# Two transformer blocks on one core: from one common order of steps to an order for each engine

## The chip, the cores and the metric

The kernel runs on one core of a Trainium2 chip. The core has TensorE (PE in the views; its weight loads are PEld), VectorE (DVE), ScalarE (ACT), GpSimd (POOL), and SyncE (SP), which here only issues DMAs. The engines run their own instruction streams and meet at semaphores. The metric is the device time of one execution in microseconds (us); less is better.

## The reference

Input is one sequence of 256 tokens with 2048 channels, all in fp32, which goes through two blocks. The first mixes with sparse attention (NSA: compressed, selected and window branches, 8 query heads, 2 key heads) and a gated DeltaNet (8 heads), merges the two, and ends in a feed-forward net (FFN). The second mixes with RWKV7 (16 heads of 64) and latent attention (MLA, 8 heads), and ends in an FFN with a convolution in its gate. Cut to the steps that matter:

```python
# block 1
h = rms_norm(x, norm1_w);  proj = h @ w_in
o_nsa = nsa_mixer(q, kv, gates)                # 3 branches, softmax each
o_dn  = gated_deltanet(qkv, z, a, beta)        # conv of 4 taps, silu, l2norm, chunks, triangular solve
mixed = g_nsa * (o_nsa @ w_up_nsa) + g_dn * (o_dn @ w_up_dn)
x = x + mixed @ w_o
x = x + (silu(h2 @ w_gate) * (h2 @ w_up)) @ w_down;  x = rms_norm(x, norm_f_w)
# block 2
proj = rms_norm(x) @ w_in_2
y = concat(rwkv7_mixer(...), mla_mixer(...))   # a recurrence; softmax attention
x = x + y @ w_out
x = x + (silu(conv3(h @ w_gate)) * (h @ w_up)) @ w_down;  return rms_norm(x)
```

## The kernel before

**Main stream.** All weights pass once through a ring of 6 blocks of 128 x 1024 fp32 elements. ACT copies the high part of each block (`split`, L1413, recorded at the helper's L1290), DVE subtracts it to get the low part (`split`, L1911, recorded at L1798, tile `ringl`), each 3 blocks ahead (`AHEAD`). PE multiplies each 128 x 128 weight tile twice: a matmul of 512 columns with the high part (both halves of the activation) and one of 256 with the low part (L732). There are 904 blocks, made by `plan`, numbered in the order of use; a "unit" is one output tile of 128 channels, and units take PSUM banks 0, 1 and 2 in turn. What leaves a bank: `evac0`, `evac1` and `evac2` on ACT (L1320, L1383, L1395), DVE (L1836, L1870, L1897) and POOL, called for the units that ended one, two and three blocks ago. Weights come by DMAs that SP issues, as ring slots come free.

**Sums into x.** Units of `wo`, `down` and `wout` are added to x by DVE (two adds, and a subtract for the low part, `low_of` L1809). For the next norm ACT then does `taken_in` (L1292): the high copy of x and one or two squares, which POOL adds up and PE sums over channels (`sums`, L737). `evac0` of ACT calls `taken_in` in the visit that follows the end of the unit, ahead of the next `split` copy on ACT:

```python
if u.kind in ("down", "wout", "wo"):
    if summed_in(u):
        e.wait_ge(mdve.sem, mdve.after("free", u.i))
        taken_in(summed_in(u), key[-1])
    return
```

**Side work.** Gates, the DeltaNet (4 groups of 2 heads), NSA (4 groups of query heads and times, 12 turns), RWKV (8 pairs of heads in 2 streams) and MLA (4 turns) run between the tiles of the main stream. Each is a generator per engine, cut at named steps; a table (`DELTA`, `RECUR`, `attention()` and so on) gives each step two numbers, what it costs PE and how long its other engines take. `arrange` (L337) walks the main sequence, and gives each step one place in it. `weave` (L325) then runs, on every engine, that engine's share of the step at that same place in its own main work; an engine without a share has an empty `yield`. A stream's next step is placed when its latency is over by the model. Side work has PSUM banks 3 to 7. NSA turns alternate between banks 3 and 4 in a single stream; the MLA has bank 7. The DeltaNet's convolutions belong to its DVE generator, and start after group g-1's "on" step.

**Halts.** At four places (`up0` block 118, `up1` 166, `out0` 600, `out1` 616) the main stream needs a mixer's output: the steps that are left run first, then ACT and DVE split the mixer's output (`parts_of_y`, L1313 and L1825, tile `yur`). In time: the mixers of block 1 lie from about 30 to 725 us, its FFN to 1705, the mixers of block 2 to 2357, `wout`'s second half to 2415, its FFN to the end.

Of the kernel before, what the change touches and what calls it, by code (L numbers as in the profile page):

```python
# [12 lines left out]
AX = mybir.AxisListType  # L13
# [17 lines left out]
TILE, TILE4, TILE33, ROWS = 0.346, 0.432, 0.426, 0.72  # L31
INVERSE = [(f"inv{lev}{x}", 0.9, 1.0) for lev in range(1, 6) for x in "ab"] \
    + [("invt", 0.5, 1.2), ("inv6a", 0.9, 1.0), ("inv6b", 0.9, 1.4)]
GATES = [("tr", 0.3, 0.8), ("act", 0.0, 3.0), ("sp", 0.0, 6.0), ("cs", 0.3, 2.0)]
DELTA = [("conv0", 0.0, 3.4), ("conv1", 0.0, 3.4), ("conv2", 0.0, 3.4), ("silu", 0.0, 5.2), ("ss", 1.8, 2.5), ("nrm", 0.0, 10.0),
         ("gb", 0.9, 5.5), ("kk", 1.8, 2.4), ("lt", 0.5, 1.1), ("vk", 0.7, 0.7), ("inv0", 0.0, 2.6)] + INVERSE \
    + [("r0", 0.5, 0.9), ("s", 0.5, 0.9), ("kgs", 0.5, 1.5), ("r1", 0.5, 0.9), ("o", 1.4, 2.8), ("on", 0.9, 1.0), ("fin", 0.0, 6.0)]
RECUR = [("mix", 0.0, 3.2), ("lw", 1.8, 2.6), ("dec", 0.0, 1.8), ("kk", 0.5, 2.4), ("nrm", 0.0, 3.4), ("rk", 0.5, 2.2),
         ("exp", 0.0, 2.4), ("ar", 0.0, 2.4), ("rows", 1.2, 0.2)] + 4 * [("p", 0.9, 0.5)] + [("l", 0.9, 1.0), ("inv0", 0.0, 2.0)] + INVERSE \
    + 2 * [("G", 0.6, 0.7), ("sa", 0.4, 0.9), ("o", 1.2, 0.8)] + [("mean", 0.5, 1.4), ("var", 0.5, 1.0), ("fin", 0.0, 4.0)]  # L40
# [121 lines left out]
def plan(banks):  # L162
# [142 lines left out]
class Side:  # L305


    seen = {}

    def __init__(self, name, steps, places):  # L310
        self.name, self.steps, self.places, self.n, self.names = name, steps, places, 0, []

    def next(self):
        return self.places[self.n] if self.n < len(self.places) else 1e10

    def step(self):
        self.names.append(next(self.steps))
        self.n += 1

    def close(self):  # L320
        assert next(self.steps, None) is None, (self.name, len(self.places))
        assert Side.seen.setdefault(self.name, self.names) == self.names, self.name


def weave(main, sides):  # L325

    for at in itertools.chain(main, [1e9]):
        while True:
            s = min(sides, key=Side.next)
            if s.next() > at:  # L330
                break
            s.step()
    for s in sides:
        s.close()


def arrange(atoms, sides):  # L337

    now, i, late = 0.0, 0, 0
    ready, places = {s: 0.0 for s in sides}, {s: [] for s in sides}

    def met(needs):
        return all(len(places[s]) >= n for s, n in needs)
    while i < len(atoms) or any(len(places[s]) < len(sides[s]) for s in sides):
        place, cost, needs, gap = atoms[i] if i < len(atoms) else (1e8, 0.0, [], None)
        stuck = i == len(atoms) or not met(needs)
        if stuck and gap is not None:
            place = gap + 1e-3 * late  # L350
        can = [s for s in sides if len(places[s]) < len(sides[s]) and sides[s][len(places[s])][2] <= place
               and met(sides[s][len(places[s])][3])]
        s = min(can, key=ready.get) if can else None
        if s is not None and (stuck or ready[s] <= now):
            step = sides[s][len(places[s])]
            now = max(now, ready[s]) + step[0]
            ready[s] = now + step[1]
            places[s].append(place)
            late += stuck
        else:  # L360
            assert not stuck, (i, {s: len(places[s]) for s in sides})
            now += cost
            i, late = i + 1, 0
    return places


def build(nc, known=None):
# [17 lines left out]
    with ctx:  # L385
# [46 lines left out]
        gpe, gact, gdve = count("s_gate_pe"), count("s_gate_act"), count("s_gate_dve")  # L432
        dpe, dact, ddve, dpool = count("s_dn_pe"), count("s_dn_act"), count("s_dn_dve"), count("s_dn_pool")
# [56 lines left out]
        mxb, smb = ar.take(4), ar.take(4)  # L490
# [48 lines left out]
        mxb2, smb2 = ar.take(4), ar.take(4)  # L539
# [30 lines left out]

        gaps = [mark["up0"], mark["up1"], mark["out0"], mark["out1"]]

        def P(m):
            return m + sum(50 for at in gaps if at <= m)

        def done(*key):

            return P(units[index[key]].end()) + 1.75  # L580

        def attention():

            out = [("rq", 0.9, 1.6, done("q", 2 * g + 1)) for g in range(4)]
            out += [("rkc", 0.9, 2.0, done("kc", 1)), ("Bkc", 0.0, 2.5, 0), ("rks", 0.9, 1.6, done("ks", 1)),
                    ("rkw", 0.9, 1.6, done("kw", 1)), ("hkc", 0.0, 1.8, done("cmpkc")), ("tkc", 0.0, 1.4, 0), ("ckc", 0.3, 0.8, 0),
                    ("Bvc", 0.0, 2.5, done("vc", 1)), ("hvc", 0.0, 1.8, done("cmpvc")), ("tvc", 0.0, 1.4, 0), ("cvc", 0.3, 0.8, 0)]
            for n in range(4):
                i = n % 2
                for br in range(3):  # L590
                    out += [("s", 0.9, 1.0, 0)] * (2 if br and i else 1)
                    nk = 64 if br == 0 else 512 * (i + 1)
                    out[-1] = ("s", 0.9, 0.8 + 0.0025 * nk, 0)
                    out += [("sm1", 0.0, 0.5 + 0.0009 * nk, 0), ("sm2", 0.0, 1.0 + 0.0022 * nk, 0)]
                    out += [("t", 0.5, 0.9, 0)] * (2 if br and i else 1)
                out.append(("o", (2.7, 4.4)[i], 0.5, done("vw")))
            return out

        def latent_attention():
            out = [("lat", 1.8, 5.0, done("lat", 7)), ("lat", 1.8, 5.0, 0)]  # L600
            out += [("rq", 0.9, 1.6, done("uq", 11)), ("rq", 0.9, 1.6, 0), ("rk", 0.5, 2.4, done("uk", 7))]
            for n in range(4):
                i = n % 2
                out += [("s", 1.8, 1.0, 0)] * (1 + i)
                out[-1] = ("s", 1.8, 0.8 + 0.0025 * 512 * (1 + i), 0)
                out += [("sm1", 0.0, 1.0 + 0.4 * i, 0), ("sm2", 0.0, 2.1 + 1.1 * i, 0)] + [("t", 0.5, 0.9, 0)] * (1 + i)
                out.append(("o", 0.9 + 0.9 * i, 0.5, done("uv", 3)))
            return out

        sides = {"gates": [(a, b, done("dn", 0, 0, 0), []) for _, a, b in GATES], "dn": [], "nsa": [], "lora": [], "mla": []}  # L610
        for g in range(4):
            for name, a, b in DELTA:
                first = {"conv0": ("dn", g, 0, 1), "conv1": ("dn", g, 1, 1), "conv2": ("dn", g, 2, 1), "o": ("dn", g, 3, 1)}.get(name)
                sides["dn"].append((a, b, done(*first) if first else 0, [("gates", len(GATES))]))
        sides["nsa"] = [(a, b, first, [("gates", len(GATES))]) for _, a, b, first in attention()]
        sides["lora"] = [(0.0, 8.0, P(mark["main2"]) + 1.0, []), (0.0, 3.0, done("lora", 2), []), (0.0, 1.0, 0, [])]
        for s in range(STREAMS):
            sides[f"rw{s}"] = [(a, b, done("rw", q, 2) if name == "mix" else 0, [("lora", 3), ("mla", 2 if name == "fin" and q >= 4 else 0)])
                               for q in range(s, 8, STREAMS) for name, a, b in RECUR]
        turns_of_last = [(f"rw{s}", (8 // STREAMS - 1) * len(RECUR) + 2) for s in range(STREAMS)]  # L620
        sides["mla"] = [(a, b, first, turns_of_last if name == "o" else []) for name, a, b, first in latent_attention()]

        names = [n for n, _, _ in DELTA]
        nsa_names = [a[0] for a in attention()]
# [3 lines left out]
                 mark["up0"]: [("nsa", len(sides["nsa"]))], mark["up1"]: [("dn", len(sides["dn"]))],  # L628
                 mark["uq"]: [("mla", 2)],
                 mark["out0"]: [(f"rw{s}", len(sides[f"rw{s}"])) for s in range(STREAMS)],  # L630
                 mark["out1"]: [("mla", len(sides["mla"]))]}
        for g in range(2, 4):
            needs[units[index[("dn", g, 0, 0)]].first()] = [("dn", (g - 2) * len(names) + names.index("conv2") + 1)]
            needs[units[index[("dn", g, 3, 0)]].first()] = [("dn", (g - 1) * len(names))]
# [2109 lines left out]
```

## Time and profile before

| | |
|---|---|
| median of 3 runs (lowest, highest) | 3183.57 us (3171.96, 3190.08) |
| profiled execution: time | 3187.08 us |
| profiled execution: span, mean granted clock | 3185.3 us, 0.969 |
| PE busy | 2978.0 us, 93% |
| DVE busy | 2064.2 us, 65% |
| ACT busy | 1362.6 us, 43% |
| POOL busy | 358.8 us, 11% |
| moved by DMA | 476.13 MB, mean 149 GB/s |

A busy time is the sum of an engine's own instructions over the profiled execution; matmul ends are modelled, so that a busy PE is not PE at its peak. The granted clock is the share of full speed that the chip gave TensorE.

### The profile page before, as it was taken

Reading aid. Unit: us, or ns where it says so; the run is one execution under the profiler, and the core shown is the slowest. Engines: PE = TensorE matmul, PEld = TensorE weight load, DVE = VectorE, ACT = ScalarE, POOL = GpSimd, SP = SyncE. Lnnn points to the kernel's source line nnn. Section 1 sums busy time; section 2 is a strip of 40 time slices with the busy share of each in tenths; the row PEclk is TensorE's granted clock in tenths of the full one; section 3 lists DMA queues with packets and bytes.
Section 4 is the critical chain, followed back from the end, with each engine's and each line's share of the span. In section 5 each row is a group of like instructions: output and inputs, shape, how many; then the busy total and the mean of one; then the engine's idle time right before and its main releaser. Section 6 shows DMA issues by size and latency. Waiting matters only on the chain.

```text
span 3185.3 us, 42727 instructions
## 1 busy us (share of the span) xinstructions
PE 2978.0 (93%) x16976; PEld 2581.7 (81%) x16976; DVE 2064.2 (65%) x3115; ACT 1362.6 (43%) x2052; POOL 358.8 (11%) x404
## 2 busy tenths in 40 slices
PE   7999988899999999999998888889998999999998
PEld 6778777788888888888876777778877888888886
DVE  6685567666666666656667756666566777756655
ACT  5352334345554444444445332333345444434434
POOL 2121001110011111001012100000001111101101
PEclk9999889999999999999999998999999999999999
DMA  5343322255555555555554211212234555555554
GB/s 202 106 153 133 114 71 93 101 190 173 188 183 188 187 186 185 186 187 188 187 165 163 92 60 60 86 67 73 90 136 152 186 187 188 186 185 186 186 177 153
DMA packets 132246, 476.13 MB, mean 149 GB/s; under 512 B 14672, under 2 KB 14928, under 8 KB 131792
## 3 DMA queue, kind: packets, MB, share of 16 engines
q1 hardware_dynamic: 132048, 473.40, 43.1%
q8 instruction: 136, 2.23, 0.3%
q14 instruction: 62, 0.51, 0.1%
HBM read 471.24 MB, written 2.10 MB: 149 GB/s over the span
## 4 chain that ended last, share of the span: by engine, by line
PE 78%; DVE 15%; ACT 5%; issue 2%; POOL 0%; DMA 0%; DVEq 0%; ACTq 0%; SPq 0%; POOLq 0%
PE ps L732 77%; DVE ringl L1798 5%; DVE U L1798 3%; ACT high L1290 2%; DVE U L1807 2%; DVE xT L1798 1%; PE ps L735 1%; DVE U L1804 1%; DVE U L2063 1%; DVE hr L1807 1%; POOL U L2508 0%; ACT U L1290 0%; ACT U L1303 0%; DVE U L2354 0%; DVE U L2423 0%
## 5 line engine op out<-in xcount | busy, mean ns | idle before, releaser
L732 PE MATMUL ps<-hr,high 128*128 128x512 f32 x4688 | 1725.5, 410 | 40.4 <-DVE ringl L1798 35.2
L1798 DVE TENSOR_TENSOR ringl<-ring,high 128x1024 fp32r<-128x1024 f32 x882 | 1092.3, 1240 | 548.3 <-ACT high L1290 546.0
L732 PE MATMUL ps<-hr,ringl 128*128 128x256 f32 x4688 | 1327.6, 283 | 0.0
L1290 ACT ACTIVATE high<-ring 128x1024 fp32r<-128x1024 f32 x882 | 912.9, 1039 | 629.1 <-PE ps L732 618.3
L732 PEld LDWEIGHTS ps<-hr,high 128*128 128x128 f32 x4688 | 895.5, 191 | 257.9 <-DVE ringl L1798 27.1
L732 PEld LDWEIGHTS ps<-hr,ringl 128*128 128x128 f32 x4688 | 899.5, 192 | 6.0 <-issue 3.9
L732 PE MATMUL ps<-yur,high 128*128 128x512 f32 x2176 | 782.1, 400 | 37.0 <-DVE yur L1798 21.3
L732 PE MATMUL ps<-yur,ringl 128*128 128x256 f32 x2176 | 615.2, 283 | 0.0
L732 PEld LDWEIGHTS ps<-yur,high 128*128 128x128 f32 x2176 | 411.7, 189 | 143.7 <-DVE ringl L1798 46.1
L1290 ACT ACTIVATE U<-ps 128x256 f32<-128x256 f32 (+3 forms) x494 | 181.0, 377 | 801.5 <-PE ps L732 715.0
L2508 POOL TENSOR_TENSOR U<-U,rs 128x256 f32<-128x256 f32 x293 | 270.9, 925 | 2129.8 <-DVE U L1798 2088.7
L732 PEld LDWEIGHTS ps<-yur,ringl 128*128 128x128 f32 x2176 | 412.1, 189 | 0.1
L732 PE MATMUL ps<-U 128*128 128x64 f32 (+3 forms) x2128 | 324.9, 297 | 57.3 <-DVE U L1798 36.1
L732 PEld LDWEIGHTS ps<-U 128*128 128x128 f32 x2128 | 291.2, 203 | 94.5 <-DVE U L1798 41.7
L1798 DVE TENSOR_TENSOR U<-U,ps 128x256 f32<-128x256 f32 (+1 forms) x405 | 168.1, 416 | 286.5 <-ACT U L1290 222.0
L2508 POOL TENSOR_TENSOR U<-U 128x256 f32<-128x256 f32 (+2 forms) x82 | 70.3, 864 | 611.4 <-ACT U L1303 570.9
L1798 DVE TENSOR_TENSOR xT<-xT,ps 128x256 f32<-128x256 f32 x256 | 107.3, 419 | 42.2 <-PE ps L732 37.8
L1798 DVE TENSOR_TENSOR U<-ps,cst 128x256 f32<-128x256 f32 (+1 forms) x155 | 67.3, 453 | 82.9 <-PE ps L732 77.3
L1807 DVE SCALAR_TENSOR_TENSOR U<-U 128x256 f32<-128x256 f32 (+4 forms) x237 | 108.3, 457 | 10.0 <-ACT U L1410 3.5
L1807 DVE SCALAR_TENSOR_TENSOR U<-U,cst 128x256 f32<-128x256 f32 (+1 forms) x239 | 107.1, 484 | 3.6
L1290 ACT ACTIVATE hr<-xT,cst 128x256 fp32r<-128x256 f32 x64 | 31.2, 506 | 122.1 <-DVE xT L1798 80.1
L1798 DVE TENSOR_TENSOR U<-U 128x256 f32<-128x256 f32 (+6 forms) x169 | 74.5, 458 | 7.0 <-ACT U L1695 2.1
(164 smaller groups left out, 1204.5 us busy)
## 6 DMA issues: line engine op xcount, KB each, us to landing
ring<-in_w_dram SPq DMA_DIRECT2D x872, 512.0 KB, 3.3
ring<-in_w_dram SPq DMA_DIRECT2D x32, 256.0 KB, 3.2
xT<-in_x_dram SPq DMA_DIRECT2D x4, 512.0 KB, 7.8
out_dram<-hx SPq DMA_DIRECT2D x4, 512.0 KB, 3.0
cst<-in_cst_dram SPq DMA_DIRECT2D x1, 1754.5 KB, 14.2
yT<-in_lora_dram SPq DMA_DIRECT2D x1, 1024.0 KB, 5.9
U<-in_lora_dram SPq DMA_DIRECT2D x1, 512.0 KB, 3.9
posi<-in_pos_dram SPq DMA_DIRECT2D x1, 128.0 KB, 2.0
```

The costliest lines, as they stand in the source:

```text
L732: return e.matmul(out, l, r, start=start, stop=stop)
L735: return e.transpose(out, i, ident)
L1290: return e.activation(out, i, ACT.Copy, scale=scale)
L1798: return e.tensor_tensor(out, a, b, op)
L1804: return e.tensor_scalar(out, a, s1, None, op0)
L1807: return e.scalar_tensor_tensor(out=out, in0=a, scalar=s, in1=b, op0=op0, op1=op1)
L2063: e.reciprocal(tm[:, 0:4, :], tm[:, 0:4, :]).then_inc(ddve.sem, ddve.inc())
L2508: return e.tensor_tensor(out, a, b, op)
```

## The change

1. The tables list each step's parts by engine, in order (`("PE", 0.9), ("DVE", 0.45)`; `"+POOL"` is a part beside the others). `arrange` gets a main queue for each of PE, ACT, DVE and POOL and follows the four in time; it always starts what can start first, side work ahead of main work when both can, except that main work of another engine that is a block behind PE goes first. It returns an own order for each engine. An engine's generators keep only the steps in which it has work. Main evacuations are called at places m-0.5 and m.
2. NSA is a first part (`nsa_first`: rotations and compression, bank 3) and two streams with 6 turns each, one on bank 3 and one on bank 4, with own `mxb` and `smb`. MLA is `mla_first` (bank 7) and two streams, on banks 7 and 2. From `main2` (block 514) to `ffn2` (block 632) the main stream has banks 0 and 1 only.
3. The convolutions are a stream of their own on DVE with a semaphore of its own, and wait for what group g-1's "vk" and POOL's "kg" have read, not for its "on".
4. `taken_in` for units 0 to 14 of a sum moves from ACT's `evac0` to its `evac1`, one visit later; unit 15 stays.
5. In the DeltaNet the reciprocal over 1024 elements is two over 512, each a step; the scaling of Rr is done in "vk"; the tanh of z comes ahead of "o". In RWKV the product r k r_k is made in tile F ahead of the reciprocal, and its steps are named `kf`, `rk`, `nrm`, `em`.

```diff
+DELTA = [("tanh", ("ACT", 2.8)), ("silu", ("DVE", 1.7)), ("sq", ("ACT", 1.1)), ("ss", ("PE", 1.75), ("ACT", 2.5)),
+         ("rec0", ("DVE", 3.4)), ("rec1", ("DVE", 3.4)), ("nrm", ("DVE", 2.6)), ("gb", ("PE", 0.9), ("ACT", 1.9), ("DVE", 1.4)),
...
+    p.banks, p.n = banks[:2], 0
     for j, cl in enumerate((C128(RK0), C128(RK0 + 128), list(range(RK0 + 256, RK0 + 288)) + [-1] * 96)):
...
+    p.banks, p.n = banks, 0
     ffn(2, ("ffn_w_gate_2", "ffn_w_up_2", "ffn_w_down_2"))
...
+def arrange(main, sides):
+    engines = list(main)
+    free, at, given = {e: 0.0 for e in engines}, {e: 0 for e in engines}, {}
+    places = {e: {s: [] for s in sides} for e in engines}
...
+        for e in engines:
+            can = []
+            if at[e] < len(main[e]):
+                place, _, needs, _ = main[e][at[e]]
+                t = when(needs)
+                if t < 1e9:
+                    can.append((max(free[e], t), e != "PE" and here >= place + 1.0, 0, t, None))
+            for s in sides:
+                if queue[e, s] and queue[e, s][0] in armed[s]:
+                    t = armed[s][queue[e, s][0]]
+                    can.append((max(free[e], t), False, 1, t, s))
+            if can:
+                first = min(c[0] for c in can) + 0.05
+                c = min((c for c in can if c[0] <= first), key=lambda c: (not c[1], -c[2], c[3]))
+                if best is None or c[0] < best[0]:
+                    best = (c[0], e, c[4])
...
                 if u.kind in ("down", "wout", "wo"):
-                    if summed_in(u):
+                    if summed_in(u) and key[-1] == 15:
...
             def evac1(u):
                 key = u.key
-                if u.kind == "gate" and key[0] == 1:
+                if summed_in(u) and key[-1] < 15:
+                    e.wait_ge(mdve.sem, mdve.after("free", u.i))
+                    taken_in(summed_in(u), key[-1])
+                elif u.kind == "gate" and key[0] == 1:
...
-                    yield P(m - 1) + 1.0
+                    yield m - 0.5
...
                     e.wait_ge(dact.sem, dact.after("rs", 1, g))
-                    e.reciprocal(tm[:, 0:4, :], tm[:, 0:4, :]).then_inc(ddve.sem, ddve.inc())
+                    for k in range(2):
+                        e.reciprocal(tm[:, 2 * k:2 * k + 2, :], tm[:, 2 * k:2 * k + 2, :]).then_inc(ddve.sem, ddve.inc())
+                        yield f"rec{k}"
...
+            def convs():
                 for g in range(4):
                     R = raw[g % 2]
                     for s in range(3):
                         if s == 0 and g:
-                            e.wait_ge(dpe.sem, dpe.after("on", g - 1))
+                            e.wait_ge(dpe.sem, dpe.after("kd", g - 1))
+                            e.wait_ge(dpool.sem, dpool.after("kg", g - 1))
...
+            def nsa(s):
+                take = turns(Rota([3 + s]))
+                S_ = Sb[s]
+                for turn in range(s, 12, 2):
...
+            def mla(s):
+                take = turns(Rota([(7, 2)[s]]))
+                for n in range(s, 4, 2):
...
+            weave(main(), [Side(n, places["PE"][n], g) for n, g in (
+                ("gates", gates()), ("dn", deltanet()), ("nsa", nsa_first()), ("nsa0", nsa(0)), ("nsa1", nsa(1)),
+                ("rw0", rwkv(0)), ("rw1", rwkv(1)), ("mla", mla_first()), ("mla0", mla(0)), ("mla1", mla(1)))])
```

## Rows read from the trace of the kernel before

**Rows 1.** Windows: stretch, us; busy us (count) PE, PEld, DVE, ACT, POOL; clock; DMA, GB/s.

```profile
30.00:725.00 695.00, 634.89 (x3662) 548.89 (x3660) 459.50 (x681) 286.85 (x421) 93.24 (x90) 0.93 0.36 125
735.00:1628.00 893.00, 893.00 (x5058) 775.41 (x5057) 551.75 (x726) 423.16 (x586) 92.36 (x116) 1.00 0.54 185
1628.00:1705.50 77.50, 67.90 (x362) 55.05 (x361) 51.74 (x72) 37.61 (x70) 16.80 (x13) 1.00 0.52 166
1705.50:1732.00 26.50, 19.32 (x104) 15.88 (x103) 19.81 (x35) 14.94 (x22) 1.93 (x3) 1.00 0.51 185
1732.00:2357.00 625.00, 546.48 (x3248) 480.94 (x3246) 410.12 (x781) 203.54 (x382) 45.93 (x50) 0.95 0.24 81
2357.00:2415.00 58.00, 48.65 (x256) 40.36 (x256) 35.24 (x60) 26.04 (x44) 8.88 (x12) 0.97 0.41 145
2415.00:2431.00 16.00, 11.76 (x54) 9.73 (x55) 11.55 (x16) 9.31 (x15) 2.76 (x4) 0.89 0.30 100
```

**Rows 2.** PE's waits, 30 to 725 us: who, total us, times, longest.

```profile
PE ps L735 <- DVE U L1798: 16.5, 8, 4.4
PE ps L732 <- DVE yur L1798: 11.0, 1, 11.0
```

**Rows 3.** PE's waits, 1732 to 2357 us.

```profile
PE ps L732 <- DVE U L1798: 27.9, 26, 3.4
...
PE ps L732 <- ACT U L1290: 9.3, 10, 2.4
```

**Rows 4.** Timeline of DVE, then PE: start, us, operation, idle before and releaser.

```profile
412.13 1.36 DVE L1798 TENSOR_TENSOR ringl<-ring,high 128x1024 fp32r<-128x1024 f32 x1 [0.52 <-ACT high L1290]
...
414.87 1.43 DVE L1798 TENSOR_TENSOR U<-U 128x4 f32<-128x4 f32 x2
...
416.45 0.87 PE L735 MATMUL ps<-cst,U 128*128 128x128 f32 x3 [3.47 <-DVE U L1798]
```

**Rows 5.** Timeline of DVE before the halt at up0.

```profile
554.22 6.55 DVE L2063 RECIPROCAL U<-U 128x1024 f32<-128x1024 f32 x1
```

**Rows 6.** Timeline of PE at the halt of out0.

```profile
2289.36 0.67 PE L732 MATMUL ps<-yur,high 128*128 128x512 f32 x1 [3.59 <-DVE yur L1798]
```

**Rows 7.** Timeline of ACT, then DVE, in one block of wout's second half.

```profile
2396.21 0.51 ACT L1290 ACTIVATE hr<-xT,cst 128x256 fp32r<-128x256 f32 x1 [2.08 <-DVE xT L1798]
2396.62 0.40 ACT L1303 ACTIVATE U<-xT 128x256 f32<-128x256 f32 x1
2396.93 1.05 ACT L1290 ACTIVATE high<-ring 128x1024 fp32r<-128x1024 f32 x1
2400.05 0.51 ACT L1290 ACTIVATE hr<-xT,cst 128x256 fp32r<-128x256 f32 x1 [2.08 <-DVE xT L1798]
...
2398.01 1.23 DVE L1798 TENSOR_TENSOR ringl<-ring,high 128x1024 fp32r<-128x1024 f32 x1 [1.44 <-ACT high L1290]
2399.15 0.87 DVE L1798 TENSOR_TENSOR xT<-xT,ps 128x256 f32<-128x256 f32 x2
2399.94 0.48 DVE L1807 SCALAR_TENSOR_TENSOR hr<-xT,cst,hr 128x256 fp32r<-128x256 f32 x1
```

**Rows 8.** Timeline of DVE in the last part of the first FFN's down.

```profile
1666.74 0.86 DVE L1798 TENSOR_TENSOR xT<-xT,ps 128x256 f32<-128x256 f32 x2
1669.40 1.36 DVE L1798 TENSOR_TENSOR ringl<-ring,high 128x512 fp32r<-128x512 f32 x1 [1.80 <-ACT high L1290]
...
1672.22 0.87 DVE L1798 TENSOR_TENSOR xT<-xT,ps 128x256 f32<-128x256 f32 x2
```

**Rows 9.** Timeline of POOL and PE at the end, before the last norm.

```profile
3167.46 0.73 POOL L2508 TENSOR_TENSOR U<-U 128x256 f32<-128x256 f32 x1 [2.26 <-ACT U L1303]
...
3170.47 1.10 PE L732 MATMUL ps<-U,cst 128*128 128x256 f32 x4 [1.91 <-ACT U L1303]
```

**Rows 10.** Tile hx on ACT, 2185 to 2272 us: min/median/max ns.

```profile
L1290 ACT ACTIVATE hx<-ps x20: 362/381/428, 2192.6 to 2269.6; 128x256 f32<-128x256 f32 x20
```

**Rows 11.** Groups of ACT's table loads: count, busy us, mean ns, idle before.

```profile
L1685 ACT ACT_TABLE_LOAD x8 | 10.3, 1283 | 0.1
```

More of the change, by code:

```diff
@@ L28 @@
 STREAMS = 2
[L31 to L37, printed above, removed]
@@ L610, in build @@
[L610 to L615, printed above, removed]
@@ L646, in build @@
                 cost = [(2 * TILE4 if name in WHOLE else ROWS) * kt]
-            atoms += [(P(m) + k / len(cost), c, needs.get(m, []) if k == 0 else [], gap if k == 0 else None)
-                      for k, c in enumerate(cost)]
-        places = arrange(atoms, sides)
+            starts, ends = p.starts.get(m, []), p.ends.get(m, [])
+            for k, c in enumerate(cost):
+                first = [u for u in starts if u.parts[0][3] // 128 * kt == k or len(cost) == 1]
+                of = ([("lo", m)] if k == 0 and m in order and m >= AHEAD else []) + ([("parts", m)] if k == 0 and m in halted else [])
+                of += (needs.get(m, []) if k == 0 else []) + [("free", before[u.i]) for u in first if before[u.i] is not None]
+                gives = [("used", m)] if k == len(cost) - 1 else []
+                gives += [("end", u.i) for u in ends if k == len(cost) - 1 or len(ends) == 2 and u is ends[0] and k == kt - 1]
+                work["PE"].append((m + k / len(cost), c, of, gives))
@@ new lines, in build @@
+        for m in range(M + 3):
+            ends = p.ends.get(m - 1, [])
+            own = [u for u in ends if not sums_x(u)]
+            both_ = [u for u in ends if not one_half(u)]
+            later = [u.kind for u in p.ends.get(m - 2, [])]
+            work["ACT"].append((m - 0.5, 0.4 * len(own) + 0.4 * (later.count("mg") + later.count("up")), [("end", u.i) for u in own],
+                                [("free" if one_half(u) else "half", u.i) for u in own] + [("data", u.i) for u in own if one_half(u)]))
+            work["DVE"].append((m - 0.5, sum(0.85 if sums_x(u) else 0.9 if u.kind == "up" else 0.43 for u in both_) + 0.4 * later.count("up"),
+                                [("end" if sums_x(u) else "half", u.i) for u in both_], [("free", u.i) for u in both_]))
+            work["POOL"].append((m - 0.5, 0.7 * len(both_), [("free", u.i) for u in both_], [("data", u.i) for u in both_]))
+            work["POOL"].append((m, 0.0, [("used", m - 1)] if 0 < m <= M else [], []))
+            x = m + AHEAD
+            split_too = x < M and x in order
+            n = blocks[x][2] * len(blocks[x][3]) / BLK if split_too else 0.0
+            hold = 2.4 if m in halted else 0.0
+            of = [("used", x - RING)] if split_too and x >= RING else []
+            of += [("used", split_[order[x] - HIGH])] if split_too and order[x] >= HIGH else []
+            work["ACT"].append((m, 1.06 * n + hold, of + (needs[m] if m in halted else []), [("hi", x)]))
+            work["DVE"].append((m, 1.23 * n + hold, [("hi", x)], [("lo", x), ("parts", m)]))
```

892 lines of the change are left out of this document (411 added, 481 removed).

## Prediction

> **What bounds the kernel now.** The page comes first: TensorE is busy 93% of the span, and no other engine above 65%. An average over unlike stages can't say where the other 7% is, so the windows view was cut at the places where PE begins or stops being full. In the first FFN (735 to 1628) PE is busy throughout at full clock, 5058 matmuls in 893.0 us, 0.1766 us each [rows 1]; it has nothing to win. Two stretches with side work are not full: from 30 to 725 PE sits idle for 695.0 - 634.9 = 60.1 us and its clock is 0.93, from 1732 to 2357 it is idle for 78.5 us at 0.95 [rows 1]. The lower clock costs about .07 x 634.9 + .05 x 546.5 = 72 us more. So mixers lose 138.6 + 72 = about 210 us, and this clock loss stands only where PE has idle pieces: 0.52 us for each idle one.
>
> Four short stretches around the ends of the sums (1628 to 1732, 2357 to 2431) lose some more [rows 1].
>
> Who is late is in PE's waits: nearly always DVE [rows 2, 3]. That engine has time to spare, 459.5 of 695 us busy [rows 1], so it is not slow but late: it does things in an order in which what PE wants stands behind something else. One such place can be read in full: at 412.13 DVE subtracts a block that PE wants three blocks later, then ends a softmax; PE waits 3.47 us for that and starts 0.15 us after DVE's last multiply ended (414.87 + 1.43 = 416.30 to 416.45) [rows 4]. At the halt before `up0` a reciprocal of 6.55 us [rows 5] stands before what PE wants, and PE waits 11.0 us [rows 2].
>
> **Part 1: the end of the sums (`taken_in`).** In `wout`'s second half each unit is one block of 8 tiles, 16 matmuls, 16 x .1766 = 2.83 us. The trace shows a block each 3.85 us (2396.21 to 2400.05): ACT waits 2.08 us for DVE's adds of the unit just ended, takes it in (.51 + .40), and only then copies the next block; DVE waits 1.44 us for that copy, subtracts, and adds the next unit, which PE has ended meanwhile [rows 7]. It is a ring of two engines that wait for each other. With `taken_in` a visit later, what it waits for is long done, and DVE's own work is all that counts: 1.23 + .87 + .48 = 2.58 us [rows 7], under 2.83. So PE sets the pace: 256 matmuls x .1766 = 45.2 us in place of 58.0 [rows 1], less 3.2 for the halt's own wait, which stays: 9.6 gained. The same ring stands in the first `down`: 12 tiles take 1672.22 - 1666.74 = 5.48 us [rows 8] where 24 matmuls take 4.24; DVE's own work is .87 + .47 and the two subtracts, 1.36 and 1.23, 3.9 us [rows 7, 8], so it fits, barely. There 362 x .1766 = 63.9 of 77.5 us: 13.6 gained. Of the two stretches that follow, 1705.5 to 1732 (96 main matmuls and 8 of sums at .28 [rows 9] need 19.2, so 7.3 lost) and 2415 to 2431 (50 and 4 need 9.9, 6.1 lost) [rows 1], the first pieces are the ring's last turns and the others the norm's own chain: half, 6.7. At the end of the program it costs: units 14 and 15 are now taken in together, so the copy and square of one (.51 + .40 [rows 7]) and part of POOL's add (.73) lie ahead of the sums that start at 3170.47 [rows 9]: 1.5. Sum: 9.6 + 13.6 + 6.7 - 1.5 = **28 us gained**. Below that the bound is 13, if `down`, with .3 us to spare, stays as it is and the tail costs double.
>
> **Part 2: own orders, streams, convolutions ahead.** No work leaves and hardly any is added; only its order changes. What remains is worked out from what can't go. In the changed code PE has 404 side steps (2 for gates, 96 DeltaNet, 45 NSA, 240 RWKV, 21 MLA). A step that comes just in time costs the handover, .15 us [rows 4], a step that comes early nothing, and a late one more; I take .15 for each: 61 us. Four halts stay, since the split of a mixer's last output can't begin before it: 3.59 us [rows 6] each, 14. That leaves 75 idle of 138.6, and with the clock's .52 for each 113 of 210: **97 us gained**. The nearest rows give the bounds: .08 for a step (half come early) leaves 46 idle, 70 in all, gain 140; .22 leaves 103, 157 in all, gain 53. Farther out nothing is gained at all, if each hidden wait is replaced by another; and at most 80% can come back, 168.
>
> Convolutions ahead and two NSA streams are in this sum: they lengthen what can be done while a chain waits for ACT and DVE. They leave the halt at `up0` without the 6.55 us reciprocal in front, now two halves.
>
> No DMA is added or moved. SP issues by free ring slots as before, at a DMA share of .24 to .36 in the mixers and .54 in the FFN [rows 1], so a faster mixer finds its weights there.
>
> **Part 3: two banks.** From `main2` to `ffn2` there are 92 units; with two banks PE may begin unit n only when n-2 has left its bank, so an evacuation has a unit's length (5.6 us for 16 tiles, 2.8 for 8). For most that is ample. In the `uq`/`uk` blocks units of 4 tiles end in pairs, and each copy takes .38 [rows 10]: the next block waits for both copies, about .5 us more than with a third bank, for 10 blocks: **5 us lost**. ACT was late with three banks too, 10 times by 9.3 us in all, 2.4 at most [rows 3]; the bounds are 0 and twice that, 19.
>
> **Sum.** 3187.1 (profiled execution) - 28 - 97 + 5 = 3067. It stands 3.5 us above the median: about **3064**.
>
> **A rule that speaks against it.** ACT loads a function table 55 times in the trace, in groups such as eight at one line, at 1283 ns each with no wait behind them [rows 11]. The new order goes by time and knows nothing of tables, so alternating streams could raise the number. The Trainium skill ("ScalarE: Activation LUTs", section "Table sets: the hidden batching unit") says that functions share a table by sets and that one should batch ACT work by set; the new order does not look at that. Its section "What ACT_TABLE_LOAD costs" puts a switch at about 2.66 us, of which 1.38 is a drain; the trace shows the 1.28 of the load and no drain. By that page R4 below would cost 73 us in place of 35.
>
> **The rivals.**
>
> *R1, waits only move.* If the model behind the new order is off by more than the .15 us of a handover, each engine still keeps its fixed order and waits elsewhere. For it: the order is as static as before, and a PE that waits for one late step holds all tiles behind it, 3.47 us at [rows 4]. Against it: DVE idles a third of the mixers. Only part 1 remains: 3187.1 - 28 + 5 - 3.5 = **3161**.
>
> *R2, the two banks (slower).* ACT and DVE now do side work ahead of main evacuations; with two banks PE stands as soon as one comes a unit late. The gain of 120 us is lost when each of the 92 units pays 1.3 us, and the time is over 0.5% (16 us) above the old when each pays 1.5: **3200** and more. For it: the 10 waits of up to 2.4 us [rows 3]. Against it: 2.8 to 5.6 us of slack for each.
>
> *R3, nearly all comes back.* DVE has the time, and the streams keep enough ready. 80% of 210: 3187.1 - 28 - 168 + 5 - 3.5 = **2993**. Against it: in the mixers the chains alone are long, and the halts stay.
>
> *R4, twice the table loads.* 55 more at 1.283 us [rows 11] are 71 us of ACT. It is busy less than half of the mixers [rows 1], so I let half fall on the path: 3064 + 35 = **3099**.
>
> **How the numbers follow.** The forecast gets .62, R1 .13, R3 .12, R4 .07, R2 .06. The forecast's own range is 3020 to 3110, from the bounds of part 2 (140 and 53). The whole range, 2980 to 3150, takes in R3's and R4's centres and the quicker third of R1's; it leaves out R2, most of R1 and R3's lower edge, .06 + .09 + .03 = .18. A change of 0.5%, 16 us, is about what can be told from none, since the three runs spread by 18. Faster by more: forecast, R3, R4 and two thirds of R1, .62 + .12 + .07 + .085 = .89; slower: R2, .06; the rest, .05, within.
>
> **What would show it.** Part 1: from the first `down` to the second FFN, PE without gaps and `hr` copies on ACT without the 2.08 us wait. Part 2: idle time of PE in the mixers halved, and its clock up to about .97 in both; the 11.0 us wait at `up0` down to 3.6. With R1 the idle time stays and its releasers change. Part 3: waits of main matmuls for ACT's copies `hx` of `uq` about .5 us, 10 times; with R2 there would be dozens between `main2` and `ffn2`. R4: count of table loads above 100. Wrong would be the whole sum if the clock stays at .93 with little idle time left: then the idle pieces do not set it, and 33 us of the 97 do not come ((138.6 - 75) x .52).

## The result, and the profile after

The changed kernel takes **3020.15 us** (median of 4 runs, 3019.74 to 3022.85) where the kernel before took 3179.14 beside it (4 runs, 3171.96 to 3190.08). The ratio is 0.9499, with a 95% interval of 0.9468 to 0.953. The prediction was 3064 with a range of 2980 to 3150: faster as forecast, inside the range and at the lower edge of the likeliest case's own 3020 to 3110, with 159 us gained where 115 (from that median) to 120 were forecast.

The page of the changed kernel, its head and busy times; DVE and ACT do what they did, PE's share has gone from 93% to 97%:

```profile
span 3018.3 us, 42748 instructions
## 1 busy us (share of the span) xinstructions
PE 2928.7 (97%) x16976; PEld 2555.2 (85%) x16976; DVE 2062.6 (68%) x3119; ACT 1366.6 (45%) x2050; POOL 366.9 (12%) x404
```

Windows of the changed kernel, cut at the ends of the same blocks as in [rows 1] (columns as there): mixers of block 1, mixers of block 2, second half of `wout`; then three pieces of the second mixers.

```profile
27.90:656.40 628.50, 614.18 (x3663) 532.33 (x3661) 455.05 (x685) 287.30 (x420) 89.45 (x90) 0.96 0.41 138
1640.50:2206.10 565.60, 531.41 (x3247) 473.89 (x3246) 415.56 (x795) 206.67 (x383) 46.00 (x43) 0.95 0.27 90
2206.10:2254.50 48.40, 45.24 (x258) 39.69 (x258) 39.75 (x67) 28.93 (x48) 14.29 (x13) 1.00 0.51 174
...
1709.30:1919.60 210.30, 209.30 (x1389) 189.02 (x1389) 165.25 (x310) 86.98 (x158) 25.53 (x24) 1.00 0.31 101
2079.20:2158.90 79.70, 60.98 (x357) 55.24 (x355) 37.62 (x61) 19.32 (x41) 0.68 (x1) 0.75 0.02 7
1962.60:2079.20 116.60, 113.91 (x700) 100.94 (x698) 79.40 (x179) 37.48 (x90) 1.82 (x3) 1.00 0.19 64
```

The first mixers went from 695 to 628.5 us, the second from 625 to 565.6 [rows 1]. PE's idle time in both went from 138.6 to 14.3 + 34.2 = 48.5 us. What remains is not spread over the steps: for 210 us in the middle of RWKV PE is idle for 1.0 us at full clock, and 18.7 us stand in one place, from 2079 to 2159, where the DMA share is 0.02 and PE's granted clock 0.75. There the main stream has run out of tiles, and RWKV's last pairs and MLA's last turns have PE for themselves; 6.0 of the 18.7 us are the halt `out0` at its end, the wait for `yur` below.

PE's waits in the first and second mixers of the changed kernel; they answer to [rows 2, 3], where the first entries were 16.5, 11.0 and 27.9 us:

```profile
PE ps L855 <- ACT U L1377: 3.5, 5, 2.4
PE ps L855 <- ACT U L1594: 2.5, 1, 2.5
PE ps L855 <- DVE U L1835: 1.9, 4, 0.6
...
PE ps L855 <- DVE U L1835: 10.8, 6, 6.4
PE ps L858 <- DVE U L1844: 6.5, 2, 5.3
PE ps L855 <- ACT yur L1377: 6.0, 1, 6.0
```

In the second half of `wout` the ring is gone. Timeline of DVE, then ACT, in the changed kernel; a block each 2226.41 - 2223.60 = 2.81 us, PE's own pace, in place of 3.85 [rows 7], and no wait of ACT ahead of its `hr` copy:

```profile
2223.60 0.88 DVE L1835 TENSOR_TENSOR xT<-xT,ps 128x256 f32<-128x256 f32 x2 [0.41 <-PE ps L855]
2224.40 0.48 DVE L1844 SCALAR_TENSOR_TENSOR hr<-xT,cst,hr 128x256 fp32r<-128x256 f32 x1
2224.79 1.22 DVE L1835 TENSOR_TENSOR ringl<-ring,high 128x1024 fp32r<-128x1024 f32 x1
2226.41 0.88 DVE L1835 TENSOR_TENSOR xT<-xT,ps 128x256 f32<-128x256 f32 x2 [0.40 <-PE ps L855]
...
2223.66 1.06 ACT L1377 ACTIVATE high<-ring 128x1024 fp32r<-128x1024 f32 x1 [1.04 <-PE ps L855]
2224.63 0.49 ACT L1377 ACTIVATE hr<-xT,cst 128x256 fp32r<-128x256 f32 x1
```

### The profile page after: what moved, and what is told of

Its sections match the earlier page's. It is cut to its first block, busy times and chain, and to the rows that moved or that the text cites. A ratio compares the mean times of both kernels' runs of the same rounds, so it can differ in the third digit from the quotient of the medians.

```text
span 3018.3 us, 42748 instructions
## 1 busy us (share of the span) xinstructions
PE 2928.7 (97%) x16976; PEld 2555.2 (85%) x16976; DVE 2062.6 (68%) x3119; ACT 1366.6 (45%) x2050; POOL 366.9 (12%) x404
## 4 chain that ended last, share of the span: by engine, by line
PE 93%; DVE 4%; ACT 1%; issue 1%; DMA 0%; POOL 0%; DVEq 0%; ACTq 0%; SPq 0%; POOLq 0%
PE ps L855 92%; PE ps L858 1%; DVE ringl L1835 1%; DVE U L1835 1%; DVE U L1844 0%; ACT high L1377 0%; DVE hr L1844 0%; ACT U L1377 0%; POOL U L2517 0%; DVE hx L1835 0%; DMA xT<-in_x_dram 0%; DVE xT L1835 0%; DVE yur L1835 0%; DVE rs L1855 0%; DVE U L2432 0%
## 5 line engine op out<-in xcount | busy, mean ns | idle before, releaser
L855 PE MATMUL ps<-hr,high 128*128 128x512 f32 x4688 | 1689.7, 404 | 25.6 <-DVE ringl L1835 18.8
L1835 DVE TENSOR_TENSOR ringl<-ring,high 128x1024 fp32r<-128x1024 f32 x882 | 1078.8, 1225 | 460.1 <-ACT high L1377 459.6
L855 PEld LDWEIGHTS ps<-hr,high 128*128 128x128 f32 x4688 | 885.0, 189 | 238.2 <-issue 21.9
L1835 DVE TENSOR_TENSOR U<-U,ps 128x256 f32<-128x256 f32 x405 | 167.9, 416 | 231.5 <-ACT U L1377 191.0
L855 PE MATMUL ps<-U 128*128 128x64 f32 (+4 forms) x2128 | 305.2, 291 | 15.5 <-ACT U L1377 6.6
L855 PEld LDWEIGHTS ps<-U 128*128 128x128 f32 (+1 forms) x2128 | 278.8, 197 | 47.5 <-issue 11.3
L2517 POOL TENSOR_TENSOR U<-U 128x256 f32<-128x256 f32 (+2 forms) x82 | 81.4, 998 | 579.7 <-ACT U L1390 523.3
L1844 DVE SCALAR_TENSOR_TENSOR U<-U,cst 128x256 f32<-128x256 f32 x239 | 107.5, 486 | 3.6
L1835 DVE TENSOR_TENSOR U<-U 128x256 f32<-128x256 f32 (+7 forms) x169 | 75.0, 460 | 8.3 <-ACT U L1745 2.9
L855 PE MATMUL ps<-U,ring 128*128 128x256 f32 (+1 forms) x288 | 62.6, 367 | 0.7 <-ACT hx L1377 0.6
```

Of the source, the lines that this page charges most:

```text
L855: return e.matmul(out, l, r, start=start, stop=stop)
L1835: return e.tensor_tensor(out, a, b, op)
L1844: return e.scalar_tensor_tensor(out=out, in0=a, scalar=s, in1=b, op0=op0, op1=op1)
L2517: return e.tensor_tensor(out, a, b, op)
```

## The experiments

Each has four runs, and its median is given. "Changed kernel" is 3020.2; e1 is compared with the kernel before beside it. One program's runs lie up to 13 us apart (e9: 3011.6 to 3021.6; e12: 3012.6 to 3026.0), those of the kernel before up to 18, and the first FFN's 272 blocks, whose code no edit below touches but e1's and e2's, took 747.1 us in some traces and 743.4 in others (e4, e7, e11, e12). So differences under 10 us between two medians are read from the stretches of the traces.

**e1: the kernel before, with `taken_in` one visit later.**

```diff
-                    if summed_in(u):
+                    if summed_in(u) and key[-1] == 15:
...
             def evac1(u):
                 key = u.key
-                if u.kind == "gate" and key[0] == 1:
+                if summed_in(u) and key[-1] < 15:
+                    e.wait_ge(mdve.sem, mdve.after("free", u.i))
+                    taken_in(summed_in(u), key[-1])
+                elif u.kind == "gate" and key[0] == 1:
```

> The kernel before with one edit alone: units 0 to 14 of a sum are taken in one visit later on ACT. If the two engines' ring at the ends of the sums is a cost of its own, it gives here what the traces of the two kernels differ by there, 13.7 in the first down, 6.7 and 6.7 in the stretches behind the sums and 9.6 in the second half of wout: about 37 us, 3142. The prediction's own figure was 28, 3151. Rival: the wait only moves to another place of the old order, and less than 10 us come, 3170 or more.

3154.89 (before 3174.07), ratio 0.9928 (0.9906 to 0.995): by the ratio 16 to 30 us gained, about 23; by the medians 19, less than the 37 and the 28 expected. In its windows the first FFN, which ends in `down`, has the changed kernel's 747 us, and the second half of `wout` (third line) nearly its 48.4:

```profile
938.80:1686.00 747.20, 747.19 (x4230) 648.44 (x4228) 458.78 (x602) 354.27 (x494) 88.55 (x101) 1.00 0.57 186
1686.00:1711.50 25.50, 21.07 (x104) 17.19 (x104) 20.34 (x35) 14.00 (x22) 2.26 (x3) 0.93 0.58 209
...
2336.00:2385.70 49.70, 46.58 (x257) 40.64 (x258) 39.81 (x66) 28.91 (x48) 14.36 (x13) 0.97 0.52 170
```

The stretch behind `down`, 25.5 us against 26.5 [rows 1], stays slow here; in the changed kernel it is 20.0. So some 5 of the 37 us that I had put down to this edit are the new order's. Against the trace of the kernel before, the stretches gain 29 us here: the first FFN (760.8 to 747.2), the one behind it (26.5 to 25.5), the second half of `wout` (58.0 to 49.7) and the second FFN (753.5 to 747.0).

**e2: the changed kernel, with `taken_in` in the first visit again** (e1's edit the other way round).

> The changed kernel with taken_in back in the first visit for all units. If the two parts add up, the ring comes back whole: 37 us, 3057, and the first down takes 761 us from the end of block 242 to the end of block 514 again in place of 747. Rival: the new order keeps DVE's adds ahead of ACT anyway, and the time stays within 10 us of 3020.

3049.80: 30 us lost. The ring comes back, with gaps on PE of 9.5 and 12.0 us:

```profile
874.20:1634.90 760.70, 751.22 (x4229) 648.34 (x4227) 463.08 (x602) 352.95 (x493) 88.45 (x101) 1.00 0.56 183
...
2221.80:2284.40 62.60, 50.56 (x256) 41.39 (x256) 37.47 (x63) 27.86 (x47) 9.62 (x13) 0.95 0.41 135
```

13.6 and 14.2 us lost in these two. The part is worth 30 us in the new order; in the old one the stretches say 29 and the times 16 to 30 (e1).

**e3: one common order.** The walk in time stays, but each step gets one place for all engines, that of PE's next main tile when its first part began.

```diff
...
+        begun.setdefault((s, n), (here, number))
+        places[e][s].append(((s, n), name))
...
+    most = 0.0
+    for key, (at_pe, count) in sorted(begun.items(), key=lambda x: x[1][1]):
+        most = max(most, at_pe)
+        begun[key] = (most, count)
+    for e in engines:
+        for s in sides:
+            places[e][s] = [(begun[key], name) for key, name in places[e][s]]
...
-                    yield m - 0.5
+                    yield m - 0.001
```

> The changed kernel, where each step has one place for all engines again (that of PE's next main tile when the step's first part was begun by the same walk in time); streams, convolutions and costs are the changed ones. If it is the own order of each engine that took the waits away, most of the 128 us of the mixers come back: 3100 to 3150. Rival: the streams and the convolutions ahead did it, or the walk over four engines, and one common order is as good: 3040 at most.

3121.66: 101 us lost, within the expectation of the first theory. Windows of the two mixers:

```profile
28.70:696.00 667.30, 620.77 (x3663) 532.70 (x3661) 455.93 (x685) 288.13 (x420) 93.53 (x90) 0.96 0.39 130
1681.40:2306.20 624.80, 551.71 (x3247) 486.21 (x3245) 414.76 (x794) 203.34 (x381) 44.69 (x43) 0.92 0.25 81
```

The second mixers are back at 624.8, as slow as before the change [rows 1]; in the first, 28 of the 67 us stay. PE waits for DVE and ACT again (the longest sums of the first mixers, then of 1640 to 2306 us):

```profile
PE ps L863 <- ACT U L1602: 9.2, 4, 3.6
...
PE ps L863 <- DVE U L1843: 16.7, 12, 5.5
```

An engine's share of a step that lies at PE's place stands behind, or ahead of, whatever that engine has at this place. The 101 us are the price of this one common order; no other way to place the steps in common was tried.

**e4: flat costs.** The walk plans with 1.0 us for every part of a side step.

```diff
+        sides = {s: [(n, [(e, 1.0) for e, _ in x], w) for n, x, w in v] for s, v in sides.items()}
         places = arrange(work, sides)
```

> The changed kernel, planned with 1.0 us for every part of every step of side work in place of its table's duration; the main stream's costs stay. If the order must follow true durations, as rival R1 of the prediction held, steps come late by a us or more and a third or more of the mixers' gain goes: 3060 or more. Rival: what can start goes first is enough, and durations hardly matter: within 15 us of 3020.

3140.32: 120 us lost, 92 of them in the first mixers (720.4 us) and 28 in the second (593.7); this is rival R1's mechanism at work. PE's longest waits in the first mixers, and one of the four behind the first of them (timeline of DVE, then PE):

```profile
PE ps L856 <- DVE U L1842: 22.2, 4, 5.9
PE ps L859 <- DVE U L1836: 16.2, 8, 5.0
PE ps L856 <- ACT U L1595: 14.3, 4, 6.5
```

```profile
473.57 6.57 DVE L2104 RECIPROCAL U<-U 128x512 f32<-128x512 f32 x2 [4.18 <-ACT U L1600]
480.05 1.16 DVE L1836 TENSOR_TENSOR ringl<-ring,high 128x1024 fp32r<-128x1024 f32 x1
481.13 0.41 DVE L1836 TENSOR_TENSOR U<-U,ps 128x256 f32<-128x256 f32 x1
481.46 1.22 DVE L1845 SCALAR_TENSOR_TENSOR U<-U 128x1024 f32<-128x1024 f32 x1
...
484.60 1.19 PE L856 MATMUL ps<-U,cst 128*128 128x512 f32 x1 [5.89 <-DVE U L1842]
```

The plan took the two halves of the DeltaNet's reciprocal for 2.0 us; they take 6.57. So PE's next step of the group stands too early in its order, and the main tiles behind it wait with it, 5.89 us.

**e12: flat costs, but true ones for DVE's long parts.**

```diff
+        sides = {s: [(n, [(e, d if e == "DVE" and d >= 2.0 else 1.0) for e, d in x], w) for n, x, w in v]
+                 for s, v in sides.items()}
```

> As the run with 1.0 us for every part of the side work, which took 3140, but with the true durations for DVE's parts of 2 us and more (9 steps of the DeltaNet and RWKV, 52 times in all, beside the convolutions, rotations and softmaxes of that length). If the order needs to know only where DVE is long away, most of the 120 us lost come back: 3060 at most. Rival: it is the many short parts, taken for 1.0 in place of 0.35 to 0.9, that put steps in the wrong order: 3100 or more.

3020.01, the changed kernel's own time. All 120 us come back. Its windows:

```profile
28.60:659.60 631.00, 607.29 (x3663) 529.63 (x3661) 453.49 (x685) 288.75 (x420) 92.14 (x90) 0.97 0.42 137
1640.90:2203.50 562.60, 527.82 (x3246) 472.64 (x3246) 414.06 (x793) 213.95 (x389) 42.95 (x43) 0.96 0.28 90
```

The mixers' stretches agree too: 631.0 + 562.6 here, 628.5 + 565.6 in the changed kernel. The order has to know when DVE is away for 2 us and more. All other parts stood at 1.0 us, not only the many short ones but also PE's and ACT's long ones (up to 4.4 and 2.9 us in the tables), and nothing was lost by that.

**e5: NSA in one chain of turns.**

```diff
+                    if n_ == "s" and t and name == "nsa":
+                        needs.append(turns_[name, "t", t - 1] if br else turns_[name, "o", n - 1])
```

> The changed kernel, planned so that each turn of NSA begins when the turn before it has ended (one chain in turns on banks 3 and 4, as before the change). In the changed kernel the last NSA turn ends near 427 us and the halt that needs it is at 479, so one chain has some 50 us to spare; but while a turn waits for its softmax, PE must have something else. If the second stream is what fills PE there: 10 to 20 us lost, 3030 to 3040, as idle time between 306 and 480 us. Rival: the DeltaNet and the main stream fill it as well, within 5 us of 3020.

3038.37: 18 us lost, but not where I expected it. PE is full up to the block before the halt, and comes there at 462.5, earlier than with two streams (479); the loss is behind it, with 15.3 us idle at a clock of 0.91:

```profile
306.80:462.50 155.70, 155.21 (x948) 134.24 (x948) 123.60 (x207) 72.15 (x106) 23.27 (x22) 0.99 0.40 136
462.50:673.30 210.80, 195.51 (x1109) 169.46 (x1108) 133.69 (x186) 93.28 (x142) 23.32 (x23) 0.91 0.36 120
```

The main stream used its tiles up while NSA was slow, and NSA's last turn ended at 498 us, past the halt, with nothing left to fill PE.

**e6: convolutions not ahead.**

```diff
-        sides["cv"] = [(f"conv{j}", [("DVE", 3.0)], need(("dn", g, j, 1), *ready_) + ([("dn", (g - 1) * len(names) + names.index("inv0"))] if g else []))
+        sides["cv"] = [(f"conv{j}", [("DVE", 3.0)], need(("dn", g, j, 1), *ready_) + ([("dn", (g - 1) * len(names) + names.index("on") + 1)] if g else []))
```

> The changed kernel, planned so that the convolutions of a DeltaNet group begin only after the step on of the group before, as before the change. That puts 9 us of DVE work back into the chain of each of groups 1 to 3, 27 us in all. PE is full from 320 to 656 us but for some 7 us. If the DeltaNet's chain sets the halt at 656: 10 to 27 us lost, 3030 to 3047. Rival: PE's own work sets it and main tiles fill the 27 us: within 5 us of 3020.

3027.73: 7.6 us, between the two figures and less than the 13 us by which one program's runs can lie apart. The trace bears a small loss out: the first mixers take 631.7 us in place of 628.5, with 13.5 us of idle time from the halt `up0` to `up1` in place of 5.8. But it is not the DeltaNet's chain that comes late at `up1`; 13.2 us are one wait at `up0`, 0.7 in the changed kernel, where DVE does one half of a reciprocal (3.35 us) and two convolutions (3.1 us each) between PE's last main matmul and the split that PE wants:

```profile
501.55 0.77 PE L855 MATMUL ps<-yur,high 128*128 128x512 f32 x1 [13.16 <-DVE yur L1835]
```

**e7 and e9: MLA in one chain, with three banks and with two.**

```diff
+                    if n_ == "s" and t and name == "mla":
+                        needs.append(turns_[name, "o", t - 1])
...
-    p.banks, p.n = banks[:2], 0
...
-    p.banks, p.n = banks, 0
...
-                take = turns(Rota([(7, 2)[s]]))
+                take = turns(Rota([7]))
...
+                    if n:
+                        e.wait_ge(aact.sem, aact.after("o", n - 1))
...
-                bank = (7, 2)[s]
+                bank = 7
```

(e9 has the first two lines alone.)

> The changed kernel with the MLA in one chain of turns on bank 7, and three banks for the main stream all through. By the prediction the third bank is worth 5 us in the uq and uk blocks, by rival R2 far more; the trace of the changed kernel shows PE waiting 0.6 us for hx copies in all there, so that I expect nothing from the banks. The MLA's turns end near 2132 and are needed at 2206, so one chain, some 15 us longer, should cost nothing either: within 3 us of 3020. Rival: the chain of MLA pushes work into the tail of RWKV, 10 us or more lost.

> The changed kernel with the MLA in one chain of turns, and two banks from main2 to ffn2 as in the change. The same with three banks took 3005.6, 15 us less than the changed kernel. If the third bank gave that, as the prediction's part 3 has it with its bound of 19, this one stays at 3020 (3017 to 3024). Rival: the single chain gave it, since it runs MLA's turns later, where RWKV leaves gaps: 3005 to 3009.

With three banks 3005.55, with two 3021.29. So MLA's second stream is worth nothing, and the third bank is. By the medians it is 16 us, though one run of each lies apart from its other three (3014.4 with three banks, 3011.6 with two). The two profiled executions are 17 us apart; 3.7 of these lie in the first FFN, where both programs are alike, and in the second mixers it is 563.5 against 554.6, 9 us:

```profile
1641.50:2081.00 439.50, 423.99 (x2638) 378.45 (x2637) 345.24 (x687) 170.99 (x327) 44.35 (x42) 0.98 0.28 96
2081.00:2205.00 124.00, 105.95 (x612) 95.33 (x611) 70.33 (x108) 38.04 (x58) 0.68 (x1) 0.85 0.20 68
```

```profile
1636.10:2065.40 429.30, 416.08 (x2593) 371.85 (x2592) 339.35 (x673) 167.48 (x324) 46.55 (x43) 0.99 0.29 99
2065.40:2190.70 125.30, 108.36 (x657) 97.69 (x655) 75.76 (x121) 36.05 (x57) 0.68 (x1) 0.88 0.20 68
```

The first pair of rows is e9's, the second e7's. My expectation for e7 was wrong. One place where the bank counts can be read, behind the first FFN: with two banks PE waits 6.4 us there for DVE to empty a bank (read in full further down, under part 2), with three only 4.1, and for the low part of a block (e7's trace):

```profile
1642.99 0.80 PE L855 MATMUL ps<-hr,high 128*128 128x512 f32 x1 [4.08 <-DVE ringl L1837]
```

**e8: RWKV ahead of MLA** when both can start on an engine.

```diff
-                c = min((c for c in can if c[0] <= first), key=lambda c: (not c[1], -c[2], c[3]))
+                c = min((c for c in can if c[0] <= first), key=lambda c: (not c[1], -c[2], (c[4] or "")[:3] == "mla", c[3]))
```

> The changed kernel, where MLA steps come behind the other side steps when several can start on an engine. The last stretch with idle time, 2079 to 2159 (18.7 us idle and a clock of half speed for 44 us), is the end of RWKV's last pairs with no main tile left. If MLA's steps took PE from RWKV just before, RWKV ends earlier and MLA fills its gaps: 8 to 15 us gained, 3005 to 3012. Rival: RWKV's last pairs wait for their own handovers only, not for PE: within 3 us of 3020.

**3004.11**, ratio to the kernel before 0.9445 (0.9425 to 0.9466): 16 us better than the changed kernel, and with e7 (3005.55) the best version here. The second mixers take 550.3 us in its windows, with 10.4 us idle behind the last block of `uv` in place of 18.7, 6.5 of them the halt `out0`:

```profile
1640.60:2100.30 459.70, 441.39 (x2782) 393.91 (x2783) 354.42 (x707) 170.91 (x335) 44.60 (x43) 0.99 0.27 92
2100.30:2190.90 90.60, 80.25 (x467) 70.67 (x465) 60.75 (x89) 36.33 (x49) 0.00 (x0) 0.91 0.28 94
```

**e10: both, e8's order and e7's banks and chain.**

> Both changes that gained 15 us by themselves: MLA behind RWKV in the order of each engine, and MLA in one chain with three banks for the main stream. If they fill the same gaps at the end of RWKV, hardly more comes: 2998 to 3006. If one of them is the banks, they add up: 2986 to 2993.

3007.13, 1 us above the first figure's range. They do not add up. The second mixers take 550.2 us, as in e8: the third bank with the single chain brings nothing more once RWKV goes first.

**e11: as e10, with the sines and cosines behind the first FFN in three steps.**

```diff
-        sides["lora"] = [("lora0", [("DVE", 5.8), ("ACT", 2.2)], [("used", mark["main2"] + 3)]),
+        sides["lora"] = [("lora0", [("DVE", 2.6)], [("used", mark["main2"] + 3)]), ("lsin", [("DVE", 2.7), ("ACT", 1.7)], []),
+                         ("lcos", [("DVE", 3.1), ("ACT", 0.5)], []),
...
```

> The kernel of the run before in this list (RWKV first, MLA in one chain, three banks), with the 18 DVE operations for the sines and cosines behind the first FFN as three steps in place of one. In the changed kernel's trace they run in one go from 1638.0 to 1646.4 and PE waits 6.4 us for the low part of a block behind them, at half clock for some us after. If the length of a step is what PE waits for: 5 to 9 us less than the run before. Rival: PE waits for DVE's other work there as well and 3 us come at most.

3019.24: 12 us lost in place of 5 to 9 gained. The edit did what it was for where it was made: PE's wait behind the first FFN fell from 4.7 us in e10 to 2.4 in all. Up to the end of `uv`'s blocks it is quicker than e10 (409.4 us against 426.7), behind them slower (149.9 against 123.5), with 24.0 us idle:

```profile
1641.40:2050.80 409.40, 401.76 (x2498) 358.45 (x2497) 320.25 (x627) 161.43 (x312) 46.77 (x41) 1.00 0.30 103
2050.80:2200.70 149.90, 125.86 (x750) 112.47 (x748) 95.82 (x168) 41.50 (x69) 1.09 (x2) 0.87 0.16 57
```

It looks like e5's lesson once more, that main tiles which are used early are missing at the end; this is argued. Why the new plan came out this way (the edit changes the order of all that follows) was not tried apart.

## Why the prediction was right, and where its sizes were off

**Reading, right.** The loss stood where the windows put it, in the two mixers and at the ends of the sums; the FFNs gave nothing else. The mixers' waits were waits for DVE's order, not for DVE's speed: its busy time did not change (2064.2 to 2062.6), and one common order put back costs 101 us (e3).

**Part 1, right in mechanism, and in size with some luck.** 28 us forecast, 30 by e2, 16 to 30 by e1. The two terms read from the ring's periods came out closely: 13.6 forecast for `down` and 13.7 in the changed kernel, 9.6 for `wout` and 9.6 (8.3 in e1, 14.2 in e2). The stretches behind gave 6.5 and 6.7 where I took half of each, 6.7 in all; e1 shows that some 5 us of it belong to the new order. The 1.5 us at the end was not seen: from the last main matmul to the end of the span both kernels take 16.8 us. In the changed kernel's trace the terms thus come to 36.5 us; that 28 lies so near e2's 30 is in part luck.

**Part 2, right in mechanism, too small in size: the step that failed is "I take .15 for each: 61 us".** 97 us were forecast and 66.6 + 59.0 = 126 came. Of 138.6 us idle I left 75; 48.5 remain. What was wrong is that a step costs PE a handover. It does so only when PE has nothing else, as at 416.45 [rows 4], where the order held a tile back behind the step. In RWKV's middle, with a main tile always ready, 210 us pass with 1.0 us idle. The price of the rest has to be read elsewhere: from the places where the fill runs out (12.7 us from 2079 to the halt `out0`) and where DVE does one long thing ahead of what PE wants (6.4 us at 1647, for the sines and cosines).

The halts' sum was right, their sizes and their place were not. I had four of 3.59 us, 14, and the changed trace has 0.7, 3.5, 6.0 and 3.2. But those at `up1` and `out1` begin where the two mixers' windows end (28.7 to 656.4 and 2206.1), as in the kernel before, so they were no part of the 138.6, and that at `out1` was counted in part 1 as well. In the windows 6.7 of the 48.5 us are halts, and 41.8 stand for what I had put at 61.

The clock's term did not hold as I had it. I took .52 us of clock loss for each idle one, and 33 us back with 64 of idle time. PE's busy time fell by 36 us (634.9 + 546.5 to 614.2 + 531.4) with 90 of idle time gone, where .52 would give 47. By the granted clock itself it is less still: 0.93 to 0.96 in the first mixers, but 0.95 before and after in the second, though idle time there fell from 78.5 to 34.2 us; by the working that gave 72 us (.04 x 614.2 + .05 x 531.4) 51 remain, and 21 came back. So the sign "about .97 in both" failed in the second mixers, where the low clock stands in a few places (0.75 from 2079 to 2159). What the other 15 us of busy time are was not tried apart. Of the 29 us by which the whole came out better than forecast, 26 are idle time.

Of the other signs, idle time fell by more than half in both, PE's wait at `up0` from 11.0 to 0.7 where I had 3.6, and the `hx` waits were one, not ten.

Timeline of DVE, then PE, at 1647 in the changed kernel (the DVE operations from 1638.05 to 1646.4 are left out but for the first):

```profile
1638.05 2.24 DVE L2278 CAST U<-posi 128x256 f32<-128x256 int32 x1
...
1646.42 0.42 DVE L1835 TENSOR_TENSOR U<-U,ps 128x256 f32<-128x256 f32 x1
1646.76 1.22 DVE L1835 TENSOR_TENSOR ringl<-ring,high 128x1024 fp32r<-128x1024 f32 x1
...
1646.99 0.77 PE L855 MATMUL ps<-hr,high 128*128 128x512 f32 x1 [6.44 <-DVE U L1835]
```

PE starts 0.15 us after DVE has read a bank out (1646.42 + 0.42 = 1646.84), and before the split that follows has ended (1647.98). So it waited for the bank, not for a block's low part, as I had it in the expectation of e11: with two banks the next unit needs the bank that DVE empties only behind the sines and cosines.

**Which piece of it.** Own orders 101 us (e3), the sums' end 30 (e2), NSA's second stream 18 (e5), the convolutions 3 to 8 (e6), MLA's second stream none (e9 against the changed kernel), and the two banks a loss. Each was taken from the changed kernel alone, and they overlap, so that their sum of 152 to 157 lies near the 159 in part by chance. Item 5 of the change was not tried by itself.

**Part 3, too small but within its bound, and its place wrong.** I had 5 us with a bound of 19; the stretches of e7 and e9 say 9, the medians 16. But PE waits for `hx` copies only once, 0.6 us, in the changed trace: it takes side steps of MLA in the meantime. Some 2 us stand behind the first FFN, 6.4 against 4.1 (e7). A likely way to the rest is that main tiles and RWKV's steps come later by it, since the loss vanishes in e10 where RWKV goes first; that is argued, not shown.

**The rivals.** R1 did not come, but e4 shows that it was near: with wrong durations the same walk loses 120 us and ends at 3140. The tables were good enough, and by e12 only DVE's parts of 2 us and more had to be. R2 did not come: the two banks cost 9 to 16 us, not 125. R3 (2993) was nearer than the forecast, 27 us off against 44: of its 168 us of the mixers' 210, 126 came. R4 did not come: 53 table loads against 55, still 1283 ns each with hardly a wait before them (one of the groups: columns as in [rows 11]):

```profile
L1741 ACT ACT_TABLE_LOAD x8 | 10.3, 1283 | 0.1
```

That column is the idle time before a load; the prediction read it as the wait behind. What comes behind shows in the timeline of ACT in the kernel before, where the next operation starts 0.01 us after the load:

```profile
1723.20 1.28 ACT L1310 ACT_TABLE_LOAD   x1
1724.49 0.48 ACT L1310 ACTIVATE U<-ps,cst 128x256 f32<-128x256 f32 x1
```

The orders that the new walk makes have 51 (e3, e7, e11) to 59 loads (e12), and e12's six more than the changed kernel's cost nothing (3020.01). The rule of the Trainium skill ("ScalarE: Activation LUTs", section "Table sets: the hidden batching unit"), to batch ACT's work by table set, thus had no case here.

**What bounds it now.** The second mixers seem to be as long as RWKV's chain of four pairs in each of two streams, though PE is 94% busy in them: they got 15 us shorter when MLA's steps stood back (e8), and where main tiles were used earlier the end was bare (e11). That is argued from these two; how short the chain would be by itself was not tried.

## What to carry to other kernels

When engines run in a fixed order, give each its own, built by following all of them in time, and measure the long operations for it: here 101 us hung on the separate orders and 120 on the durations of VectorE's parts of 2 us and more, while all other parts could be taken as 1.0 us at no loss. Price what remains by where the fill runs out, not by a handover for each step; and after such a change look at which chain ends the stage, and let that chain go first wherever two can start (16 us here).

## What the runs showed of the hardware that was not expected

PE's granted clock fell to 0.75 on the mean, between its two levels of 1.2 and 2.4 GHz, from 2079 to 2159 us, where PE was busy for 61.0 of 79.7 us with small matmuls of side steps alone; it stood at 1.00 from 1709 to 1920, where main tiles lay between the same kinds of steps and PE was never idle for long. And the first FFN's 272 blocks took 747.1 us in some executions and 743.4 in others, with the same code, PE full and its granted clock 1.00 in both. No wait makes the difference but PE's own pace: from 1000 to 1500 us it ran 2850 matmuls in e7's trace and 2832 in the changed kernel's. What sets this was not tried.
